# Norm roots and scalings of three mixers, placed between the difference heads of a two-layer attention stage

## The chip, the cores and the metric

The kernel runs on one core of a Trainium2 chip. The metric is the device time of one execution in microseconds (us); several runs are taken and their median counts. The engines are called as the profile calls them: PE is TensorE (PEld its weight loads), DVE is VectorE, ACT is ScalarE, POOL is GpSimd, SP is SyncE.

## The reference

Two transformer blocks run one after the other on 512 tokens of width 1024. The first (sparse attention, a recurrent branch, a gated feed-forward) is not touched by the change. The second is run twice (two layers); each layer has a half-weight gated feed-forward, a mixer stage, another feed-forward and a norm. In the mixer stage four kinds of attention work side by side on 256 columns each, and each result is normalised before one common projection:

```python
pa, pb, pc, pd = jnp.split(h @ w_in[l], IN_SPLITS, axis=-1)
ya = neighbourhood_mixer(pa, ...)   # rms_norm over its 256 columns
yb = mla_mixer(pb, ...)             # rms_norm over its 256 columns
yc = diff_mixer(pc, ...)            # rms_norm over the 64 columns of each head
yd = gqa_mixer(pd, ...)             # rms_norm over its 256 columns
x = x + jnp.concatenate([ya, yb, yc, yd], axis=-1) @ w_out[l]
```

`rms_norm` divides by `sqrt(mean(x*x) + eps)`. The difference mixer (`yc`) runs two softmaxes for each of its four heads and subtracts the second, weighted, from the first.

## The kernel before, in words

Tokens are in four blocks of 128 (`TB` = 4). The function `mixers` lays all attention of one layer out as 20 groups of 4 steps, 80 steps t = 0 to 79: four latent heads (groups 0 to 3), four neighbourhood heads (4 to 7), four shared-key heads (8 to 11), and eight groups for the difference heads (12 to 19, steps 48 to 79: two per head). A step is 128 queries against up to 512 keys. `attention` (from line 938 on) turns the list into one instruction stream per engine, by hand, with semaphores between them:

- PE, in its loop at t: the scores of step t + 4 (L967), the turning of step t's probabilities (L975, transposes), and the weighing of the values for step t - 2 (L986). Turning step t waits for its exponentials and for the copy of step t - 2.
- DVE: the scores' bias and row minimum (L1065) of step t, which waits for the exponentials of step t - 3; then what `splits(dve, t)` asks for; and at every fourth t, from t = 10 on, `finish` of a group: the reciprocal of the row sums (L1033), for a second softmax its weight (L1036), and the scaled output (L1047) into `ytok` (or into `sq` for a second softmax).
- ACT: the exponentials of step t (L1016), the copy of the turned probabilities of step t - 1 out of PSUM (L1023), and then what `on_act`, here the function `squares`, asks for at t.
- POOL adds the second softmax's part to the first in `ytok` (L1080).

`ytok` holds the 1024 output columns of the 512 tokens. The norms need three steps. ACT squares a mixer's output into the tile `nabias` (L2315, at t = 44, 46 and 60; L2320 for the difference heads 0 to 2, at t = 66, 74 and 80). DVE sums the squares into columns of the small tile `ms` (L2232, at the t of the table `sums`). Then the root (ACT), the reciprocal (DVE) and the scaling of `ytok` (DVE). Before the change the roots of the three 256-column mixers (L2324) stand at ACT's t = 80, behind the last square, and their reciprocals (L2236) and the three scalings (L2241, each over 4 x 256 columns) at DVE's t = 83, behind group 18's finish and ahead of group 19's, at t = 86. Behind them comes the last difference head: its square on DVE (L2333), its sum (L2335), the roots of all four heads on ACT (L2347), reciprocal, factor and the scaling of the difference mixer's 256 columns (L2337 to L2342).

`turn_outputs` then transposes `ytok` chunk by chunk on PE (L2771, 8 chunks of 4 blocks; the six chunks of the three mixers first, the two of the difference mixer last, by `Y_ORDER`), ACT writes the high part `yhi` (L2779, 8 instructions) and DVE the low part `ylo` (L2788, 14 instructions). The projection (`products`, L388 to L390: three matmuls per chunk) starts with the first chunk whose low part is there. PE's wait for a pair of chunks is `y_normed`, raised by each scaling:

```python
for i, c in enumerate(Y_ORDER):
    pe.wait_ge(*k.y_normed.at(i // 2 + 1))
```

ACT needs a table of functions for exponentials and another for roots; the compiler puts a load (ACT_TABLE_LOAD) ahead of an activation whose function is not in the table that is loaded. Squares and copies need no change of table here.

Of the kernel before, what the change touches and what calls it, by code (L numbers as in the profile page):

```python
# [21 lines left out]
ALU = mybir.AluOpType  # L22
# [39 lines left out]
GW = 256  # L62
# [1501 lines left out]
def spread(ap, n, at=None):  # L1564

    dims = [list(d) for d in ap.ap]
    dims.insert(len(dims) if at is None else at, [0, n])
    return bass.AP(ap.tensor, ap.offset, dims)
# [561 lines left out]
def mixers(k, mem, l, near, latent, diff, shared, parted, lam, ytok):  # L2130
# [4 lines left out]
    nc = k.nc  # L2135
# [78 lines left out]
    def splits(dve, t):  # L2214
        def parts(trios, done):
            for src, hi, lo in trios:
                last = nc.vector.tensor_copy(hi, src)
            last.then_inc(*k.part_hi.up())
            dve.wait_ge(*k.part_hi.all())
            for src, hi, lo in trios:  # L2220
                last = nc.vector.tensor_tensor(lo, src, hi.bitcast(F32), ALU.subtract)
            last.then_inc(*done.up())

        def latent_head(h):
            hi, lo, khi, klo = (x[0:MD] for x in slot[h % 2])
            parts([(qB[0:MD, h, :], hi, lo), (kB[0:MD, h, :], khi, klo)], k.latent_split)

        if t in sums:
            at, squares = sums[t]
            i = list(sums).index(t)  # L2230
            dve.wait_ge(*k.y_sq.at(i + 1))
            nc.vector.tensor_reduce(k.ms[:, :, at:at + 1], squares, AX.X, ALU.add).then_inc(*k.y_sums.up())  # L2232
        if t == 83:
            dve.wait_ge(*k.y_root.at(2))
            for at, size in ((0, 2), (6, 1)):
                last = nc.vector.reciprocal(k.ms[:, :, at:at + size], k.ms[:, :, at:at + size])  # L2236
            last.then_inc(*k.y_link.up())
            dve.wait_ge(*k.y_link.at(1))
            for at, col in ((0, 0), (1, GW), (6, 3 * GW)):
                y = ytok[:, :, col:col + GW]  # L2240
                nc.vector.tensor_tensor(y, y, spread(k.ms[:, :, at], GW), ALU.mult).then_inc(*k.y_normed.up())  # L2241
        if t == -1:
            latent_head(1)
        if t in (1, 4):
            dve.wait_ge(*k.qk_done.at(ends[0 if t == 1 else 1]))
            latent_head(2 if t == 1 else 3)
        if t in (5, 9):
            c = (t - 5) // 4
            parts([(kA[:, c, :], *near_keys[c])], k.keys_split)
        if t in (8, 12, 16, 20):  # L2250
            h = (t - 8) // 4
            dve.wait_ge(*k.qk_done.at(ends[2 + h]))
            r = 64 * (h % 2)
            parts([(qA[r:r + 64, h // 2, :], slot[h % 2][0][r:r + 64], slot[h % 2][1][r:r + 64])], k.padded)
        if t == 13:
            parts([(kD[:, :], *shared_keys)], k.keys_split)
        if t in (24, 28):
            v = (t - 24) // 4
            dve.wait_ge(*k.qk_done.at(ends[6 + v]))
            r = 64 * v  # L2260
            parts([(qD[r:r + 64, j, :], slot[v][2 * j][r:r + 64], slot[v][2 * j + 1][r:r + 64]) for j in range(2)],
                  k.padded)
        if t in (30, 48):
            c = 0 if t == 30 else 1
            hi, lo, khi, klo = diff_parts[c]
            parts([(qC[:, c, :], hi, lo), (kC[:, c, :], khi, klo)], k.parted)
# [41 lines left out]
    def squares(act, t):  # L2308
        if t in (44, 46, 60):
            i = (44, 46, 60).index(t)  # L2310
            at, done = ((GW, 4), (0, 8), (3 * GW, 12))[i]
            act.wait_ge(*k.o_read.at(done))
            if i == 0:
                act.wait_ge(*k.low_done.at(32))
            nc.scalar.activation(bias[:, :, i, :], ytok[:, :, at:at + GW], ACT.Square).then_inc(*k.y_sq.up())  # L2315
        if t in (66, 74, 80):
            h = (66, 74, 80).index(t)
            act.wait_ge(*k.o_added.at(h + 1))
            act.wait_ge(*k.y_sums.at(1))
            nc.scalar.activation(head(h), maps(h), ACT.Square).then_inc(*k.y_sq.up())  # L2320
        if t == 80:
            act.wait_ge(*k.y_sums.at(3))
            for at, size in ((0, 2), (6, 1)):
                nc.scalar.activation(k.ms[:, :, at:at + size], k.ms[:, :, at:at + size], ACT.Sqrt, scale=1.0 / GW,  # L2324
                                     bias=k.eps[:, 0:1]).then_inc(*k.y_root.up())

    attention(k, groups, mem, bias_ready=(4 * TB, na_ready), ready=ready, splits=splits, on_act=squares)

    @k.block.vector
# [729 lines left out]
```

## Time and profile before

| | |
|---|---|
| median of 3 runs | 3228.33 us (3226.97 to 3229.15) |
| profiled execution | 3228.01 us |
| its span in the trace | 3226.0 us |
| PE busy | 3149.0 us, 98% of the span |
| DVE busy | 1790.4 us, 55% |
| ACT busy | 1300.7 us, 40% |
| POOL busy | 215.1 us, 7% |

The span is the time between the first and the last instruction in the trace; the profiled execution's own time has 2.0 us more around it. An engine's busy share is an average over stages; PE's high share includes the time in which it runs at the lower of its two clock levels. Times in the trace are counted from the start of the span. The mixer stage of the first layer lies at about 1572 to 1728 us, that of the second at about 2653 to 2804 us.

### The profile page before, as it was taken

Reading aid. Unit: us, or ns where it says so; the run is one execution under the profiler, and the core shown is the slowest. Engines: PE = TensorE matmul, PEld = TensorE weight load, DVE = VectorE, ACT = ScalarE, POOL = GpSimd, SP = SyncE. Lnnn points to the kernel's source line nnn. Section 1 sums busy time; section 2 is a strip of 40 time slices with the busy share of each in tenths; the row PEclk is TensorE's granted clock in tenths of the full one; section 3 lists DMA queues with packets and bytes.
Section 4 is the critical chain, followed back from the end, with each engine's and each line's share of the span. In section 5 each row is a group of like instructions: output and inputs, shape, how many; then the busy total and the mean of one; then the engine's idle time right before and its main releaser. Section 6 shows DMA issues by size and latency. Waiting matters only on the chain.

```text
span 3226.0 us, 41165 instructions
## 1 busy us (share of the span) xinstructions
PE 3149.0 (98%) x15247; PEld 2603.0 (81%) x15247; DVE 1790.4 (55%) x2676; ACT 1300.7 (40%) x1857; POOL 215.1 (7%) x238
## 2 busy tenths in 40 slices
PE   8999998999999999999999999999999999999998
PEld 6779976888888888877788888888888768888887
DVE  8367696455543555347765555345553686555532
ACT  4337765233332333233365333333322426643322
POOL 1001100010000000011201000100000021000001
PEclk9999999999999999999999999999999999999999
DMA  5340033333333333343322333333333332233332
GB/s 148 87 129 5 2 92 105 94 93 100 94 94 100 92 102 91 100 115 78 68 51 73 94 96 96 97 97 97 91 97 99 104 83 40 64 94 102 92 96 67
DMA packets 520761, 283.71 MB, mean 88 GB/s; under 512 B 40139, under 2 KB 511024, under 8 KB 520371
## 3 DMA queue, kind: packets, MB, share of 16 engines
q1 hardware_dynamic: 513154, 262.77, 29.2%
q0 software_dynamic: 5088, 17.40, 1.8%
q10 hardware_dynamic: 2384, 1.71, 0.2%
q8 instruction: 88, 1.44, 0.2%
q14 instruction: 47, 0.38, 0.0%
HBM read 268.16 MB, written 4.24 MB: 84 GB/s over the span
## 4 chain that ended last, share of the span: by engine, by line
PE 88%; DVE 7%; issue 2%; ACT 2%; DMA 1%; ACTq 0%; DVEq 0%; POOLq 0%; POOL 0%
PE bank L388 24%; PE bank L389 24%; PE bank L390 24%; PE bank L986 5%; PE bank L967 4%; PE bank L975 3%; PE bank L2491 1%; DVE wlo L364 1%; PE bank L412 0%; DVE xc L1980 0%; DVE std L2690 0%; PE bank L413 0%; PE bank L414 0%; DVE ntmp L2680 0%; PE bank L743 0%
## 5 line engine op out<-in xcount | busy, mean ns | idle before, releaser
L388 PE MATMUL bank<-hhi,whi 128*128 128x512 f32 (+1 forms) x2440 | 973.7, 399 | 5.5 <-issue 2.5
L390 PE MATMUL bank<-hlo,whi 128*128 128x512 f32 (+1 forms) x2440 | 950.5, 390 | 0.0
L389 PE MATMUL bank<-hhi,wlo 128*128 128x512 f32 (+1 forms) x2440 | 949.9, 389 | 0.0
L364 DVE TENSOR_TENSOR wlo<-raw,whi 128x1024 fp32r<-128x1024 f32 x485 | 607.5, 1255 | 551.7 <-ACT whi L357 542.7
L357 ACT CAST whi<-raw 128x1024 fp32r<-128x1024 f32 x485 | 505.0, 1047 | 399.8 <-PE bank L390 379.8
L388 PEld LDWEIGHTS bank<-hhi,whi 128*128 128x128 f32 (+1 forms) x2440 | 457.1, 187 | 117.0 <-issue 18.6
L389 PEld LDWEIGHTS bank<-hhi,wlo 128*128 128x128 f32 (+1 forms) x2440 | 457.2, 187 | 106.0 <-issue 12.0
L390 PEld LDWEIGHTS bank<-hlo,whi 128*128 128x128 f32 (+1 forms) x2440 | 457.0, 187 | 97.2
L388 PE MATMUL bank<-uhi,whi 128*128 128x512 f32 x880 | 343.0, 390 | 0.0
L390 PE MATMUL bank<-ulo,whi 128*128 128x512 f32 x880 | 342.4, 389 | 0.0
L389 PE MATMUL bank<-uhi,wlo 128*128 128x512 f32 x880 | 342.4, 389 | 0.0
L650 ACT CAST uhi<-gate 128x512 f32 x110 | 68.3, 620 | 597.2 <-DVE gate L674 597.2
L667 DVE TENSOR_TENSOR up<-bank,rinv 128x512 f32<-128x512 f32 x110 | 76.0, 691 | 288.2 <-PE bank L390 288.2
L390 PEld LDWEIGHTS bank<-ulo,whi 128*128 128x128 f32 x880 | 165.2, 188 | 34.5
L388 PEld LDWEIGHTS bank<-uhi,whi 128*128 128x128 f32 x880 | 165.2, 188 | 34.4
L389 PEld LDWEIGHTS bank<-uhi,wlo 128*128 128x128 f32 x880 | 165.2, 188 | 33.9
L1023 ACT COPY probT<-bank 128x512 f32<-128x512 f32 (+3 forms) x288 | 140.4, 487 | 85.2 <-PE bank L975 83.6
L519 POOL TENSOR_TENSOR sq<-sq 128x512 f32<-128x512 f32 x49 | 63.4, 1293 | 1644.5 <-ACT sq L537 1644.5
L975 PE MATMUL bank<-ident,prob 128*128 128x128 f32 x896 | 147.1, 275 | 1.0 <-ACT prob L1016 0.6
L677 DVE TENSOR_TENSOR ulo<-gate,uhi 128x512 f32 x110 | 76.2, 693 | 99.5 <-ACT uhi L650 99.5
L975 PEld LDWEIGHTS bank<-ident,prob 128*128 128x128 f32 x896 | 112.2, 142 | 20.7 <-ACT prob L1016 3.7
L533 ACT ACTIVATE hhi<-xT,vec 128x512 fp32r<-128x512 f32 x48 | 34.7, 724 | 172.7 <-DVE xT L602 172.7
(457 smaller groups left out, 3689.0 us busy)
## 6 DMA issues: line engine op xcount, KB each, us to landing
raw<-in_ffn_w_gate SPq DMA_DIRECT2D x88, 512.0 KB, 3.8
raw<-in_ffn_w_up SPq DMA_DIRECT2D x88, 512.0 KB, 3.7
raw<-in_w_in SPq DMA_DIRECT2D x78, 512.0 KB, 3.7
raw<-in_ffn_w_down SPq DMA_DIRECT2D x64, 512.0 KB, 3.8
raw<-in_w_out SPq DMA_DIRECT2D x24, 512.0 KB, 4.0
raw<-in_ffn_w_down SPq DMA_DIRECT2D x32, 384.0 KB, 3.3
raw<-in_w_gate SPq DMA_DIRECT2D x22, 512.0 KB, 3.8
raw<-in_w_up SPq DMA_DIRECT2D x22, 512.0 KB, 3.6
```

What stands on the lines that cost most here:

```text
L357: k.nc.scalar.copy(k.whi[:, slot, :], k.raw[:, slot, :]).then_inc(k.hi_split.sem, 1)
L364: k.nc.vector.tensor_tensor(k.wlo[:, slot, :], k.raw[:, slot, :], k.whi[:, slot, :].bitcast(F32), ALU.subtract)\
L388: mm(out, whi, hi(kc), start=start and i == 0, stop=False)
L389: mm(out, wlo, hi(kc), start=False, stop=False)
L390: last = mm(out, whi, lo(kc), start=False, stop=stop and i == kcs - 1)
L650: nc.scalar.copy(uhi[:, bass.ds(i * 2 + e, 1), :], gate[:, e:e + 1, :])\
L667: nc.vector.tensor_tensor(up[:, e, :], bank[u + 1][:, :], k.rinv[:, :], ALU.mult)\
L677: nc.vector.tensor_tensor(ulo[:, bass.ds(i * 2 + e, 1), :], gate[:, e:e + 1, :], uhi[:, bass.ds(i * 2 + e, 1), :].bitcast(F32), ALU.subtract)\
L967: last = nc.tensor.matmul(score(t), q, key, start=i == 0, stop=i == len(pairs) - 1)
L975: last = nc.tensor.transpose(k.bank[4 + t % 2][:, b * P:b * P + P], prob[:, t % 2, b * P:b * P + P], k.ident[:, :])
L986: last = nc.tensor.matmul(mixed(g)[:, e, :], probT[:, t % 3, b * P:b * P + P], v, start=b == 0, stop=b == len(values) - 1)
L1023: nc.scalar.copy(probT[:, v % 3, 0:width[v]], k.bank[4 + v % 2][:, 0:width[v]])\
```

## The change

The roots of the three 256-column mixers go from ACT's t = 80 to t = 63 (the last of their sums is made at DVE's t = 61). The reciprocals go from DVE's t = 83 to t = 66, and the three scalings, which stood one behind the other, to t = 67, 71 and 75. No arithmetic is added or left out.

```diff
-        if t == 83:
+        if t == 66:
             dve.wait_ge(*k.y_root.at(2))
             for at, size in ((0, 2), (6, 1)):
                 last = nc.vector.reciprocal(k.ms[:, :, at:at + size], k.ms[:, :, at:at + size])
             last.then_inc(*k.y_link.up())
             dve.wait_ge(*k.y_link.at(1))
-            for at, col in ((0, 0), (1, GW), (6, 3 * GW)):
-                y = ytok[:, :, col:col + GW]
-                nc.vector.tensor_tensor(y, y, spread(k.ms[:, :, at], GW), ALU.mult).then_inc(*k.y_normed.up())
+        if t in (67, 71, 75):
+            at, col = ((0, 0), (1, GW), (6, 3 * GW))[(t - 67) // 4]
+            y = ytok[:, :, col:col + GW]
+            nc.vector.tensor_tensor(y, y, spread(k.ms[:, :, at], GW), ALU.mult).then_inc(*k.y_normed.up())
...
-        if t == 80:
+        if t == 63:
             act.wait_ge(*k.y_sums.at(3))
             for at, size in ((0, 2), (6, 1)):
                 nc.scalar.activation(k.ms[:, :, at:at + size], k.ms[:, :, at:at + size], ACT.Sqrt, scale=1.0 / GW,
```

Lines behind L2241 have a number higher by one in the changed kernel. The order of instructions is the same in both layers. ACT behind the square of the shared-key mixer (t = 60), first as it was, then as it is: L1016 are the exponentials of steps 61 to 64, L1023 the copies of steps 60 to 63.

```order
L2315 ACTIVATE nabias<-ytok 128x4x256 [waits o_read]
L1016 ACTIVATE prob<-biased,low 128x512 [waits low_done,p_turned]
L1023 COPY probT<-bank 128x512 [waits p_turned,pv_done]
L1016 ACTIVATE prob<-std,low 128x512 [waits low_done,p_turned]
L1023 COPY probT<-bank 128x512 [waits p_turned,pv_done]
L1016 ACTIVATE prob<-biased,low 128x512 [waits low_done,p_turned]
L1023 COPY probT<-bank 128x512 [waits p_turned,pv_done]
L1016 ACTIVATE prob<-biased,low 128x512 [waits low_done,p_turned]
L1023 COPY probT<-bank 128x512 [waits p_turned,pv_done]
```

In the changed kernel, from the copy of step 62 on:

```order
L1023 COPY probT<-bank 128x512 [waits p_turned,pv_done]
L2325 ACT_TABLE_LOAD
L2325 ACTIVATE ms<-ms,eps 128x4x2 [waits y_sums]
L2325 ACTIVATE ms<-ms,eps 128x4
L1016 ACT_TABLE_LOAD [waits low_done]
L1016 ACTIVATE prob<-biased,low 128x512 [waits p_turned]
L1023 COPY probT<-bank 128x512 [waits p_turned,pv_done]
```

Two roots and two table loads, one to the roots' table and one back, now stand between the copy of step 62 and the exponentials of step 64. ACT at the end of the attention, changed kernel:

```order
L2321 ACTIVATE nabias<-ytok 128x4x64 [waits y_sums,o_added]
L2345 UNCONDITIONAL_BRANCH
L2348 ACT_TABLE_LOAD
L2348 ACTIVATE ms<-ms,eps 128x4x4 [waits y_sums]
L2775 UNCONDITIONAL_BRANCH
L2780 ACTIVATE yhi<-bank,vec 128x4x8x16 [waits side_turned] x2
```

The load for the last roots stands ahead of the instruction that waits for the sums, and waits for nothing itself. Per layer ACT has two table loads more than before. DVE at the end of the attention, first as it was:

```order
L2232 TENSOR_REDUCE ms<-nabias 128x4 [waits y_sq]
L1033 RECIPROCAL scale<-bank 128x4 [waits pv_done]
L1047 TENSOR_TENSOR ytok<-bank,scale 128x4x64 [waits scale_ready]
L2236 RECIPROCAL ms<-ms 128x4x2 [waits y_root]
L2236 RECIPROCAL ms<-ms 128x4
L2241 TENSOR_TENSOR ytok<-ytok,ms 128x4x256 [waits y_link]
L2241 TENSOR_TENSOR ytok<-ytok,ms 128x4x256 x2
L1033 RECIPROCAL scale<-bank 128x4 [waits pv_done]
L1036 TENSOR_TENSOR scale<-scale,lam 128x4 [waits scale_ready]
L1047 TENSOR_TENSOR sq<-bank,scale 128x256 [waits o_added,factor_used]
```

And as it is:

```order
L2232 TENSOR_REDUCE ms<-nabias 128x4 [waits y_sq]
L1033 RECIPROCAL scale<-bank 128x4 [waits pv_done]
L1047 TENSOR_TENSOR ytok<-bank,scale 128x4x64 [waits scale_ready]
L1033 RECIPROCAL scale<-bank 128x4 [waits pv_done]
L1036 TENSOR_TENSOR scale<-scale,lam 128x4 [waits scale_ready]
L1047 TENSOR_TENSOR sq<-bank,scale 128x256 [waits o_added,factor_used]
L2330 UNCONDITIONAL_BRANCH
L2334 TENSOR_TENSOR nabias<-ytok 128x4x64 [waits o_added]
```

The finish of group 19 (L1033, L1036, L1047) now follows that of group 18 directly; the only thing between is its own wait for the weighed values.

## Rows read from the trace of the kernel before

**Rows 1.** The page: busy time of each engine.

```profile
PE 3149.0 (98%) x15247; PEld 2603.0 (81%) x15247; DVE 1790.4 (55%) x2676; ACT 1300.7 (40%) x1857; POOL 215.1 (7%) x238
```

**Rows 2.** The chain that ended last, end of layer 1's attention and projection: start, us, what.

```profile
1716.19 1.28 ACT L2324
1717.48 0.50 ACT ms L2324 x2
...
1718.29 3.50 DVE ytok L2241 x3
...
1725.13 1.24 DVE ytok L2342
...
1731.06 0.23 PE bank L388
```

**Rows 3.** Timeline of DVE, same place: start, us, engine, line, operation, out<-in.

```profile
1716.75 0.42 DVE L1047 TENSOR_TENSOR ytok<-bank,scale 128x256 f32<-128x256 f32 x1
...
1721.71 0.17 DVE L1033 RECIPROCAL scale<-bank 128x4 f32<-128x4 f32 x1
...
1726.27 6.10 DVE L2788 SCALAR_TENSOR_TENSOR ylo<-bank,vec,yhi 128x128 fp32r<-128x128 f32 x14
```

**Rows 4.** Timeline of PE, layer 1's end, then layer 2's; [idle before <- releaser].

```profile
1715.02 2.79 PE L986 MATMUL bank<-vC,probT 128*128 128x65 f32 x24
1719.57 4.37 PE L2771 MATMUL bank<-ident,ytok 128*128 128x128 f32 x24 [1.77 <-DVE ytok L2241]
1726.41 1.97 PE L2771 MATMUL bank<-ident,ytok 128*128 128x128 f32 x8 [2.47 <-DVE ytok L2342]
...
1734.30 0.39 PE L388 MATMUL bank<-yhi,whi 128*128 128x512 f32 x1
...
2795.91 3.36 PE L2771 MATMUL bank<-ident,ytok 128*128 128x128 f32 x24 [1.77 <-DVE ytok L2241]
...
2811.68 0.39 PE L388 MATMUL bank<-yhi,whi 128*128 128x512 f32 x1
```

**Rows 5.** Timeline of ACT, layer 1: copy of step 62, exponentials of step 64.

```profile
1690.28 0.56 ACT L1023 COPY probT<-bank 128x512 f32<-128x512 f32 x1
1690.74 0.72 ACT L1016 ACTIVATE prob<-biased,low 128x512 f32<-128x512 f32 x1
```

**Rows 6.** Timeline of PE, layer 1: scores of step 68, turning of step 64.

```profile
1691.93 0.48 PE L967 MATMUL bank<-hhi 128*128 128x512 f32 x1
1692.25 0.60 PE L975 MATMUL bank<-ident,prob 128*128 128x128 f32 x4
```

**Rows 7.** Timeline of ACT in the first block: a table load between other work.

```profile
445.57 1.28 ACT L1920 ACT_TABLE_LOAD   x1
446.87 0.69 ACT L1920 ACTIVATE tr<-bank,half 128x512 f32<-128x512 f32 x1
```

**Rows 8.** Timeline of PE: two gaps inside layer 1's attention.

```profile
1572.56 6.77 PE L967 MATMUL bank<-hhi 96*128 96x512 f32 x15 [2.38 <-DVEq L471]
...
1605.95 0.63 PE L967 MATMUL bank<-parted,hhi 128*128 128x256 f32 x3 [1.45 <-ACT prob L1016]
```

**Rows 9.** Windows: stretch, length, busy PE, PEld, DVE, ACT, POOL, PEclk, DMA share, GB/s.

```profile
219.00:220.40 1.40, 0.01 (x1) 0.00 (x0) 1.25 (x4) 0.71 (x2) 0.08 (x1) 1.00 0.46 187
220.40:226.00 5.60, 5.59 (x34) 4.67 (x34) 4.58 (x10) 2.19 (x4) 0.00 (x0) 1.00 0.01 3
1572.60:1580.00 7.40, 7.40 (x21) 5.79 (x22) 5.37 (x10) 1.39 (x3) 0.80 (x1) 0.54 1.00 223
1606.00:1611.00 5.00, 5.00 (x31) 5.00 (x31) 2.35 (x7) 2.79 (x6) 0.00 (x0) 0.66 0.01 3
1719.57:1723.90 4.33, 4.33 (x24) 4.13 (x24) 3.39 (x7) 0.00 (x0) 0.73 (x1) 0.63 0.00 0
1726.40:1730.00 3.60, 3.59 (x14) 3.21 (x15) 3.60 (x11) 3.60 (x6) 0.00 (x0) 0.56 0.02 5
2795.91:2799.30 3.39, 3.27 (x24) 2.57 (x24) 2.89 (x5) 0.00 (x0) 0.35 (x1) 1.00 0.00 0
```

## The prediction

> **What bounds the kernel.** I read the page first: PE is busy for 98% of the span and DVE for 55% [rows 1], so that a DVE or ACT instruction costs time only where PE waits for it. The change touches two such places in each of two layers. The chain of waits at the end of layer 1's attention shows the first [rows 2]: ACT's table load (1.28 us) and three-mixer roots (0.50), the three scalings on DVE (3.50), then group 19's finish, the last head's norm, and the last scaling (1.24), on which the last transposes wait. The timelines of DVE and PE [rows 3, 4] say what the other engines could do meanwhile. The second place is the middle of the difference heads, where the roots go; there the timelines of ACT and PE say how far ahead of PE the exponentials are [rows 5, 6]. Last I read windows for the granted clock behind PE's gaps [rows 8, 9], since both edits change a gap. Layer 2 repeats layer 1's instructions 1076.3 us later with the same durations; only the clock differs (its 24 transposes take 3.36 us against 4.37 [rows 4]).
>
> **The end of the attention: a gain.** Group 19's finish starts at 1721.71 behind the scalings [rows 3]. It needs the weighed values, whose matmuls end at 1715.02 + 2.79 = 1717.81 [rows 4], and DVE behind group 18's finish, free at 1716.75 + 0.42 = 1717.17 [rows 3]. With the scalings gone it starts at about 1717.87, **3.84 us earlier**, and everything behind it hangs on it: POOL's addition, the square, the sum, the root on ACT, the last scaling, the last eight transposes, and the low parts on DVE. Two things could be late instead. ACT must load the roots' table again, 1.28 us; the order shows that load without a wait ahead of the root that waits, so it runs from 1716.19 to 1717.47 in idle time, as the load does now [rows 2], while the last scaling starts at 1725.13 - 3.84 = 1721.29 [rows 2]. Without this cover it would cost 1.28. And PE must turn the first six chunks: they start at 1717.85, behind the weighing, and take 3.36 us (4.37 at the lower clock) [rows 4], so they end at 1721.2 (1722.2), before the last scaling's end at 1726.37 - 3.84 = 1722.53 [rows 2]. Both hide.
>
> **The middle: a cost.** After the copy of step 62, which ends at 1690.84 [rows 5], ACT loads a table (1.28), takes two roots (0.50) and loads the other table back [rows 2]. A load takes 1.30 from its start to the next start [rows 7], so the exponentials of step 64 start at about 1690.84 + 0.02 + 1.29 + 0.50 + 1.30 = 1693.95 instead of 1690.74 [rows 5] and end at 1694.67. PE turned step 64 at 1692.25, directly behind the scores of step 68 [rows 6]; it will now do so at about 1694.70. Of ACT's 3.2 us delay, 0.8 are its lead and **2.45 us** reach PE as a gap. PE works without gaps from there to the end of the weighing, so the shift stays. The reciprocals on DVE wait for the roots while DVE would wait for step 64's exponentials anyway; queued behind them are group 14's finish and the minimum of step 67, neither needed for several us. The three scalings (3.50 / 3 = 1.17 each) go one by one where DVE is ahead of ACT (its minimum of step t waits only for the exponentials of step t - 3); I cost them at nothing. That cover, the minima made ahead, would have to be gone for 1.17 each. Nothing moves on the DMA queues: SP's and POOL's streams are unchanged.
>
> **The clock.** In front of the middle the granted clock is at its upper level (2.4 GHz). What a gap does to it varies. Behind gaps of 2.38 and 2.47 us PE got 0.54 of full speed for 7.4 us and 0.56 for 3.6 us; behind one of 1.45, 0.66 for 5.0; behind 1.77, once 0.63 for 4.3 and once 1.00; behind 1.40, 1.00 [rows 4, 8, 9]. Lost work, (1 - clock) x length: 3.4, 1.6, 1.7, 1.6, 0, 0 us. My new gap of 2.45 is nearest to the first two; I take **1.7**, the value of three of those six (1.6 to 1.7), and keep 0 and 3.4 as the bounds. PE is the bound there, so it is paid in full.
>
> At the end the change removes the first gap (1.77) and shortens the second: from 1721.2 to 1722.55, 1.35 us. The nearest row, 1.40, left the clock up, so I take the upper level. What that gives back is capped by DVE: the low parts end 1726.27 + 6.10 = 1732.37 [rows 3], and the last chunk's three matmuls (0.23 each [rows 2]) would let the next unit start at 1733.1; it starts at 1734.30 [rows 4]. So 1.2 in layer 1. In layer 2, 1076.3 us later, the same point is 2809.4 against 2811.68 [rows 4]: 2.2. Bounds: 0 if the clock falls as before, and these values.
>
> **The sum.** Per layer -3.84 + 2.45 + 1.7 = +0.3 us; two layers +0.6; clock at the ends -1.2 - 2.2 = -3.4; in all -2.8 us. The profiled execution took 3228.01, so I expect **3225.2 us**. It stands 0.3 below the median of the runs shown, 3228.33, within their scatter. A measurement of this kernel tells about 0.2% (6.5 us) from no change; this is less.
>
> **A rule against the change.** The row of a load shows 1.28 us, and the activation behind it starts 1.30 after the load's start, in the middle of other ACT work [rows 7]. The Trainium skill, page "ScalarE: Activation LUTs", section "Table sets: the hidden batching unit", says to batch activations by table set and not by function, and the change breaks this: exponentials, roots, exponentials, roots. By the same page ("What ACT_TABLE_LOAD costs") a switch costs about 2.66 us with a drain; by that figure an estimate for the middle gap would be 5.2 us instead of 2.45, and two layers would come to +2.7. The trace's 1.30 decides; no row here shows the drain.
>
> **The rivals.**
>
> 1. *The clock stays up in the middle.* As behind 1.77 in layer 2. Then 2 x 1.7 less: -6.2, 3221.8; in one layer only, 3223.5. For it: the gap is short and the engine is dense around it. Against: both gaps of over 2.3 us had a fall behind them. 0.15 for both cases.
> 2. *The clock falls at the end too.* The weighing, the transposes and a 1.35 us gap lie close to the 1.45 that had a fall. The give-back shrinks from 3.4 to about 1.0 (the shorter gap still saves in layer 2): -0.4, 3227.6. 0.27.
> 3. *Slower: the middle costs more than the end gives.* Mechanism: the gap at step 64 puts PE at 1.2 GHz for as long as behind the 2.38 gap, 3.4 us of lost work, with the end's give-back at 1.0 as in rival 2. Per layer -3.84 + 2.45 + 3.4 = +2.0; in all +4.0 - 1.0 = +3.0, 3231.0. It turns from gain to loss once the lost work exceeds 3.84 - 2.45 = 1.39 us a layer plus what the end gives back. 0.12.
> 4. *A switch holds ACT longer than its load's row.* With a hold of twice the load's row (2 x 1.28 per switch, two switches), the gap is 2.45 + 2.57 = 5.0, and in all -2.8 + 5.1 = +2.3, 3230.3; with 3.4 of lost clock it would be 3233.7. Against it stand the 1.30 in the first block and the roots at 1717.48, directly behind the load [rows 2, 7]. This is what the skill's drain would do; 0.04.
> 5. *The end gives nothing.* If group 19's finish were held by something as late as the scalings (the chain names only them), the middle's cost would stand alone: 2 x 4.15 = +8.3, 3236.3. Nothing in the rows supports it: 0.02.
>
> **How the numbers follow.** The forecast as it stands has 0.40, the rivals 0.15, 0.27, 0.12, 0.04 and 0.02. The range goes from rival 1 (3221.8, rounded to 3222.0, since the half case is at 3223.5) to 3229.6: it takes in rival 2 and the forecast with the 1 us by which the runs scatter, and half of rival 3, and leaves out some 0.15. Faster by over 0.2%, below 3221.9, is rival 1's outer half: 0.06. Slower by over 0.2%, above 3234.8, is rival 5 and the worst of 3 and 4: 0.03. Within: 0.91.
>
> **What would show it.** In the changed profile: two table loads and two roots on ACT between a copy and an exponential in the middle; a PE gap of 2.4 to 2.5 us ahead of the turning of step 64, and a granted clock near 0.6 for some us behind it; group 19's L1033 starting about 1.1 us behind group 18's L1047 in place of 5.0; the gap of 1.77 ahead of the 24 transposes gone; the table load at ACT's end inside idle time. Wrong would be: a middle gap over 3 us (rival 4), the last root starting directly behind its table load (the cover is gone), or a stretch from the start of step 64's turning to the start of the projection that is not some 3.8 us shorter at equal clock.

## The result, and the profile after

The changed kernel takes **3232.46 us** in the median of 22 runs (3223.98 to 3251.21), against 3226.28 (3223.36 to 3232.93) of the kernel before in as many runs beside it: 1.0028 times as long, 95% interval 1.0015 to 1.0041. (The ratio with its interval is estimated from all the runs; that of the two medians is 1.0019. So it is with the ratios below.) That is slower by a small amount that the interval keeps clear of no change, where no measurable change was forecast, and the median lies outside the range given (3222.0 to 3229.6). The profiled execution of the changed kernel took 3239.04 us.

The page of the changed kernel, its span and the busy time of each engine, against [rows 1]:

```profile
span 3237.1 us, 41171 instructions
PE 3159.9 (98%) x15247; PEld 2612.9 (81%) x15247; DVE 1793.9 (55%) x2676; ACT 1306.3 (40%) x1861; POOL 215.9 (7%) x238
```

PE has the same 15247 matmuls and is busy for 10.9 us more. ACT has four instructions more (its four table loads, two a layer) and 5.6 us more. So the extra time is mostly in matmuls that run longer, not in waits.

First the place that the edit fills, the middle of layer 1's difference heads. ACT's timeline of the changed kernel (start, us, engine, line, operation, out<-in, count), against [rows 5]:

```profile
1688.00 0.57 ACT L1023 COPY probT<-bank 128x512 f32<-128x512 f32 x1
1688.59 1.28 ACT L2325 ACT_TABLE_LOAD   x1
1689.88 0.49 ACT L2325 ACTIVATE ms<-ms,eps 128x8 f32<-128x8 f32 x2
1690.39 1.28 ACT L1016 ACT_TABLE_LOAD   x1
1691.69 0.72 ACT L1016 ACTIVATE prob<-biased,low 128x512 f32<-128x512 f32 x1
```

And PE's timeline of it, against [rows 6] (the bracket is PE's idle time before the row, and what ended it):

```profile
1692.46 0.66 PE L975 MATMUL bank<-ident,prob 128*128 128x128 f32 x4 [2.32 <-ACT prob L1016]
...
1694.37 0.77 PE L967 MATMUL bank<-hhi 128*128 128x512 f32 x1
1694.94 1.05 PE L975 MATMUL bank<-ident,prob 128*128 128x128 f32 x4
...
1697.36 0.77 PE L967 MATMUL bank<-hhi 128*128 128x512 f32 x1
...
1700.34 0.77 PE L967 MATMUL bank<-hhi 128*128 128x512 f32 x1
```

The gap is 2.32 us. Behind it the scores take 0.77 in place of 0.48, four turnings 1.05 in place of 0.60, and from one step's scores to the next's it is 2.98 to 2.99 us (1694.37, 1697.36, 1700.34). Windows of the changed kernel say for how long: the two stretches behind the gaps (layer 1, layer 2), then the two stretches from the copy of step 62 to the copy of step 79.

```profile
1693.00:1710.10 17.10, 17.10 (x78) 16.01 (x77) 7.62 (x20) 7.93 (x14) 0.73 (x1) 0.50 0.33 94
2779.00:2792.70 13.70, 13.70 (x63) 12.79 (x63) 6.54 (x17) 5.89 (x12) 0.73 (x1) 0.52 0.38 113
1688.00:1723.68 35.68, 33.36 (x215) 31.52 (x215) 16.73 (x47) 23.44 (x41) 1.46 (x2) 0.76 0.22 60
2773.17:2807.22 34.05, 31.73 (x215) 30.01 (x215) 16.63 (x47) 23.43 (x41) 1.46 (x2) 0.80 0.23 63
```

The same two stretches in the kernel before, copy to copy:

```profile
1690.28:1715.27 24.99, 24.99 (x215) 24.07 (x215) 12.79 (x42) 20.40 (x36) 1.48 (x2) 1.00 0.32 86
2766.60:2791.60 25.00, 25.00 (x215) 24.08 (x215) 12.79 (x42) 20.42 (x36) 1.47 (x2) 1.00 0.31 85
```

The last three numbers of a row are the granted clock, the DMA share and the GB/s. The same 215 matmuls take 24.99 us at a clock of 1.00 before; afterwards PE is idle for 2.32 of 35.68 us and busy for 33.36, at 0.76 on average. During 17.1 us PE was busy without a pause and was granted 0.50 of full speed, the lower level (1.2 GHz). The middle cost 10.69 us in layer 1 and 9.05 in layer 2; the forecast was 4.15 in each.

Then the end of the attention. DVE's timeline of the changed kernel, the finishes of groups 18 and 19, against [rows 3]:

```profile
1725.15 0.42 DVE L1047 TENSOR_TENSOR ytok<-bank,scale 128x256 f32<-128x256 f32 x1
1726.25 0.18 DVE L1033 RECIPROCAL scale<-bank 128x4 f32<-128x4 f32 x1 [0.67 <-PE bank L986]
```

ACT's timeline there, the table load and the last roots, against [rows 2]:

```profile
1724.60 1.28 ACT L2348 ACT_TABLE_LOAD   x1
1728.84 0.31 ACT L2348 ACTIVATE ms<-ms,eps 128x16 f32<-128x16 f32 x1 [2.96 <-DVE ms L2336]
```

PE's timeline there and at the same place of layer 2, against [rows 4]:

```profile
1723.42 2.79 PE L986 MATMUL bank<-vC,probT 128*128 128x65 f32 x24
1726.05 2.79 PE L2772 MATMUL bank<-ident,ytok 128*128 128x128 f32 x24
1730.96 1.09 PE L2772 MATMUL bank<-ident,ytok 128*128 128x128 f32 x8 [2.12 <-DVE ytok L2343]
...
1737.95 0.39 PE L388 MATMUL bank<-yhi,whi 128*128 128x512 f32 x1
...
2814.51 1.09 PE L2772 MATMUL bank<-ident,ytok 128*128 128x128 f32 x8 [2.13 <-DVE ytok L2343]
...
2822.82 0.39 PE L388 MATMUL bank<-yhi,whi 128*128 128x512 f32 x1
```

Group 19's reciprocal starts 1.10 us behind group 18's L1047, where it was 4.96 [rows 3]; the load ends 2.96 us before the roots that need it; the 24 transposes follow the weighing with no gap and take 2.79 in place of 4.37 [rows 4]. From the copy of step 79 to the next unit of the projection it is 1737.95 - 1723.68 = 14.27 us, against 1734.30 - 1715.27 = 19.03: **-4.76**, with -5.04 forecast. In layer 2 it is 2822.82 - 2807.22 = 15.60 against 2811.68 - 2791.60 = 20.08: **-4.48**, with -6.04 forecast. In this pair of profiles the two middles cost 19.7 us where 8.3 were forecast, and the two ends gave 9.2 where 11.1 were. So most of what went wrong lies behind the middle gap, and a smaller part at the end, where the last gap is 2.12 and 2.13 us and not the 1.35 of the prediction.

### The profile page after: what moved, and what is told of

Same layout as the page of the kernel before. It is cut to its first block, busy times and chain, and to the rows that moved or that the text cites. A ratio compares the mean times of both kernels' runs of the same rounds, so it can differ in the third digit from the quotient of the medians.

```text
span 3237.1 us, 41171 instructions
## 1 busy us (share of the span) xinstructions
PE 3159.9 (98%) x15247; PEld 2612.9 (81%) x15247; DVE 1793.9 (55%) x2676; ACT 1306.3 (40%) x1861; POOL 215.9 (7%) x238
## 4 chain that ended last, share of the span: by engine, by line
PE 88%; DVE 7%; issue 2%; ACT 2%; DMA 1%; ACTq 0%; DVEq 0%; POOLq 0%; POOL 0%
PE bank L388 24%; PE bank L390 24%; PE bank L389 24%; PE bank L986 5%; PE bank L967 4%; PE bank L975 3%; PE bank L2492 1%; DVE wlo L364 1%; DVE xc L1980 0%; PE bank L412 0%; DVE std L2691 0%; PE bank L413 0%; PE bank L414 0%; ACT prob L1016 0%; PE bank L743 0%
## 5 line engine op out<-in xcount | busy, mean ns | idle before, releaser
L1023 ACT COPY probT<-bank 128x512 f32<-128x512 f32 (+3 forms) x288 | 140.5, 488 | 96.7 <-PE bank L975 94.6
```

The lines of the kernel that those rows point to most:

```text
L1023: nc.scalar.copy(probT[:, v % 3, 0:width[v]], k.bank[4 + v % 2][:, 0:width[v]])\
```

## The experiments

Two explanations were open. The theory: ACT's hold opens a gap on PE, and the clock behind it falls for longer than the prediction allowed; the gap decides, whatever opens it. The rival: the table switches, or the work moved to DVE, cost by themselves. Where a kernel does more than the kernel before, what it makes in addition is read by nothing.

**Other instructions in place of the change's.** The first four kernels: the roots on DVE, the roots moved alone, and ACT held by three squares or by one, with no change of table.

e1 starts from the kernel before and takes the three mixers' roots on DVE, by eight Heron steps on the 128 x 12 means at t = 65 to 72, and the scalings at t = 73, 76 and 79; ACT's roots at t = 80 are gone (the columns of `ms` are renumbered for it, which is left out here):

```diff
+        if 64 < t <= 64 + 8:
+            linked(nc.vector.reciprocal(step, guess))
+            linked(nc.vector.tensor_tensor(step, step, half, ALU.mult))
+            linked(nc.vector.scalar_tensor_tensor(out=guess, in0=guess, scalar=0.5, in1=step, op0=ALU.mult, op1=ALU.add))
...
+        if t in (73, 76, 79):
+            i = (73, 76, 79).index(t)
...
-        if t == 80:
...
-                nc.scalar.activation(k.ms[:, :, at:at + size], k.ms[:, :, at:at + size], ACT.Sqrt, scale=1.0 / GW,
```

> The changed kernel with the three mixers' roots taken on DVE (eight steps of Heron's iteration on 12 values a partition, one per step t = 65 to 72, scalings at t = 73, 76 and 79): the table switch in the middle is gone from ACT, the end of the attention is that of the change. Theory (the gap at step 64 brings PE's clock down, and it stays down for many steps): no gap, no low stretch in the middle, the whole gain at the end stays, 3.8 to 5 us in each layer: 7 to 11 us below before. Rival (scalings and small DVE work between the heads disturb the attention in themselves): within 3 us of the changed kernel, with the turning of the steps 65 to 80 late.

Measured: 3219.27 us (3216.48 to 3234.79, 6 runs) against 3227.65 (3221.05 to 3238.45, 18 runs): 0.9968 (0.9955 to 0.9981), faster. Without a hold of ACT in the middle a gain stays. It is 8.4 us in the medians; the prediction's two ends come to 11.1.

e2 is the kernel before with the roots alone moved; reciprocals and scalings stay at t = 83:

```diff
-        if t == 80:
+        if t == 63:
             act.wait_ge(*k.y_sums.at(3))
```

> The kernel before with only ACT's roots moved to t = 63; reciprocals and scalings stay at t = 83. So it has the middle's cost and almost nothing of the end's gain (the scalings no longer wait for the roots behind the last square: 1.1 us a layer). Theory: the whole loss is in the middle. From the medians, +6 for the change and about -9 for its two ends leave some +15 for two middles, so this kernel is 10 to 16 us slower than before. Rival (the gap alone, at 2.3 us a layer, with the low clock a matter of chance): +2 to +4.

Measured: 3240.26 (3236.35 to 3249.29, 6 runs), 1.0038 (1.0025 to 1.0051): the cost is that of the roots' place, without anything moved on DVE. e3 and e4 keep the roots where they were and hold ACT with squares whose result nobody reads, three of them (the cut shown) and one; e8, further down, has two:

```diff
+        if t == 63:
+            for tile in (qA, kA, qD, kC)[:3]:
+                nc.scalar.activation(tile[:, :, :], ytok[:, 0:2, 0:T], ACT.Square)
```

> The kernel before with three squares of 1024 elements a partition added on ACT at t = 63, written to tiles that nothing reads any more: ACT is held for about 3.0 us, as by the two roots and two table loads (3.1), with no table switched. Theory (it is PE's gap, whatever makes it): gap of about 2.2 us, low clock behind it, 10 to 16 us slower than before. Rival (the table switch does something beyond its time on ACT): +4 to +6 only, two gaps.

> The same with one square (1.06 us) in place of three: ACT's lead is 0.8 us, so a gap of about 0.2 us. Theory: the clock stays up, 0.4 to 1 us above before. Rival (any disturbance of ACT at t = 63 brings the low clock): above +5.

Measured: e3 3239.47 (3231.33 to 3246.85, 7 runs), 1.0035 (1.0021 to 1.0048); e4 3228.91 (3221.08 to 3246.37, 13 runs), 0.9996 (0.9985 to 1.0007). Timelines of PE in e2 and in e3, layer 1, where step 64 is turned:

```profile
1690.98 0.66 PE L975 MATMUL bank<-ident,prob 128*128 128x128 f32 x4 [2.32 <-ACT prob L1016]
```

```profile
1692.70 0.66 PE L975 MATMUL bank<-ident,prob 128*128 128x128 f32 x4 [1.94 <-ACT prob L1016]
```

Windows of e2 behind both gaps, then of e3:

```profile
1692.00:1698.80 6.80, 6.80 (x32) 6.27 (x32) 3.11 (x10) 3.84 (x8) 0.73 (x1) 0.52 0.79 233
2778.00:2798.50 20.50, 20.50 (x92) 19.22 (x92) 6.83 (x21) 8.92 (x16) 0.73 (x1) 0.51 0.27 78
```

```profile
1694.00:1704.20 10.20, 10.20 (x46) 9.47 (x46) 3.70 (x13) 4.75 (x9) 0.73 (x1) 0.51 0.53 157
2779.00:2792.70 13.70, 13.70 (x63) 12.79 (x62) 4.50 (x14) 6.55 (x12) 0.73 (x1) 0.51 0.41 120
```

e3 has no change of table in the middle and costs what e2 costs. The rival in which the switch itself costs, beyond the time for which it holds ACT, falls. The two rows of e2 show one more thing: the same gap in the same kernel and the same execution was followed by 6.8 us at half clock once and by 20.5 the other time.

**The gap filled, and gaps of other lengths and places.** e5 is the changed kernel with 20 transposes of the identity matrix on PE, ahead of the turning of step 64, where PE would wait:

```diff
         def turn(t):
+            if bias_ready and t == 64:
+                for _ in range(20):
+                    nc.tensor.transpose(k.bank[7][:, 3 * P:4 * P], k.ident[:, :], k.ident[:, :])
             pe.wait_ge(*k.exp_done.at(t + 1))
```

> The changed kernel with 20 transposes of the identity, 128 x 128, added on PE ahead of the turning of step 64, into PSUM columns that nothing reads: at 0.11 us each they fill 2.2 of the 2.3 us for which PE stands still there. ACT's hold and the 2.3 us of delay are as in the change. Theory (the stillness of PE brings the clock down): no low stretch in the middle; per layer -4.8 at the end and +2.3 in the middle: about 5 us below before, some 10 below the changed kernel's median. Rival (the low clock comes with the table switch or with the DVE scalings): as the changed kernel, 6 above before.

Measured: 3224.72 (3218.45 to 3236.22, 12 runs) against 3228.18 (3221.74 to 3243.92, 35 runs): 0.9997 (0.9984 to 1.001). PE's timeline of e5 in layer 1:

```profile
1688.59 2.35 PE L973 MATMUL bank<-ident 128*128 128x128 f32 x20
1691.08 0.66 PE L978 MATMUL bank<-ident,prob 128*128 128x128 f32 x4
```

Windows of e5 behind that place, layer 1 and layer 2:

```profile
1691.00:1708.00 17.00, 16.92 (x142) 16.21 (x143) 12.84 (x33) 14.24 (x27) 0.74 (x1) 1.00 0.35 103
2765.00:2782.00 17.00, 16.86 (x142) 15.91 (x140) 12.30 (x31) 14.24 (x26) 0.73 (x1) 1.00 0.38 109
```

ACT's hold and its two table loads are still there and step 64 is as late as in the changed kernel (its turning starts 4.46 us behind the copy of step 62 in both), but in 17 us PE now gets through 142 matmuls, where the changed kernel did 78 in 17.1. Only the idle time on PE is gone, and with it the fall of the clock and the slowdown.

The profile alone would be weak evidence: it is of the second fastest of twelve executions. But the granted clock is on record for every run (to 0.001, which is 3 us of one run's span, so only means over many runs tell something). Span times mean granted clock, averaged over the runs, is 3197.7 us for the change (22 runs), 3197.1 for the change again (e11, 12 runs) and 3197.8 for e5; the rest of the span, (1 - clock) x span, is 35.7, 33.1 and 25.8 us. So the three are equal but for the clock, and e5 loses 7.3 to 9.9 us less to the lower level. This is the experiment that shows the cause.

Two reservations: the gain against the kernel before was expected at 5 us and is 3.5 in the medians, with an interval that holds no change; and e5 was not measured beside the change, of which the second measurement (e11, 0.9992 to 1.0029) overlaps with e5's interval.

e6, e7 and e9 are the kernel before with one root of 128 numbers into a spare column of `ms`, which brings a load to the roots' table and one back: at t = 38 among the shared-key heads (e6), at t = 63 (e7), and at t = 38 with a square of 1024 elements behind it (e9). The cut shows e9's edit; e6 has its first two added lines alone, and e7 the same two at t = 63.

```diff
+        if t == 38:
+            nc.scalar.activation(k.ms[:, 0, 7:8], k.eps[:, 0:1], ACT.Sqrt)
+            nc.scalar.activation(qA[:, :, :], qC[:, :, :], ACT.Square)
```

> The kernel before with one root of a constant (one value a partition, to an unused column of ms) on ACT at t = 38, among the shared-key heads, which makes two table loads: ACT is held for about 2.9 us. A step there has three score matmuls in place of one. Theory with an addition (how long the clock stays low depends on how much PE computes per step): gap of about 2 us and a low stretch of the length seen behind the other gaps there, 3 to 7 us: 2 x (2 + 2.5) = +5 to +9. Rival (the low stretch is as long anywhere in the attention): as e7.

> The same root at t = 63, among the difference heads. Theory: as the three squares of e3, +10 to +14 us. If the two positions cost the same, the length of the low stretch does not hang on the heads.

> The kernel before with two squares of 1024 elements on ACT at t = 63: a hold of about 2.0 us, less a lead of 0.8: a gap of about 1.2 us, between e4's 0.2 and e3's 2.0. Theory: the low clock follows in some executions and not in others, so that the runs scatter; median +3 to +6. Rival (any gap counts alike): +10 or more in all runs.

Measured, against 3228.18: e6 3229.17 (3226.17 to 3243.62), 1.0011 (0.9998 to 1.0023); e7 3239.99 (3231.68 to 3258.14), 1.0033 (1.0014 to 1.0051); e8 3227.06 (3223.42 to 3238.09), 0.9998 (0.9984 to 1.0011), 12 runs each. PE's timelines at the place of the hold in layer 1, of e6, of e7 and of e8:

```profile
1649.85 0.97 PE L967 MATMUL bank<-parted,hhi 128*128 128x512 f32 x3 [1.37 <-ACT prob L1016]
```

```profile
1691.94 0.66 PE L975 MATMUL bank<-ident,prob 128*128 128x128 f32 x4 [2.01 <-ACT prob L1016]
```

```profile
1691.70 0.66 PE L975 MATMUL bank<-ident,prob 128*128 128x128 f32 x4 [0.99 <-ACT prob L1016]
```

Windows of e7 behind its two gaps, then of e8 behind its first:

```profile
1693.00:1703.20 10.20, 10.20 (x45) 9.47 (x45) 3.80 (x12) 5.00 (x9) 0.73 (x1) 0.50 0.53 157
2775.00:2778.40 3.40, 3.40 (x17) 3.22 (x16) 1.10 (x4) 1.92 (x4) 0.00 (x0) 0.50 0.76 211
```

```profile
1691.70:1702.00 10.30, 10.29 (x87) 9.87 (x87) 6.20 (x19) 8.66 (x16) 0.73 (x1) 1.00 0.64 175
```

Two switches cost nothing that can be measured where the gap is 1.37 us (e6) and 11.8 us in the median where it is 2.01 (e7), of which the gaps themselves are 4.0. In e6 and e8 both layers keep the clock up behind the gap (1.37 and 1.36, 0.99 and 0.99 us), so two expectations missed: e6 was to cost 5 to 9 us, e8 3 to 6. Between 1.37 and 1.94 us no gap was made.

e6 and e7 differ in the place and in the gap, so it could still be that the fall is long only among the difference heads. e9 makes the longer gap among the shared-key heads; e11 and e12 are the changed kernel and e1 again, measured side by side; e10 is e1 with 16 more transposes of the identity on PE in the gap before the last two chunks:

```diff
         for i, c in enumerate(Y_ORDER):
+            if i == 6:
+                pe.wait_ge(*k.o_read.at(19))
+                for _ in range(16):
+                    nc.tensor.transpose(banks[6][:, 3 * P:4 * P], k.ident[:, :], k.ident[:, :])
             pe.wait_ge(*k.y_normed.at(i // 2 + 1))
```

> e6 again (a root and two table loads on ACT at t = 38, among the shared-key heads), with one more square of 1024 elements there, to a tile that nothing reads any more. e6 left a gap of only 1.4 us there, since ACT's lead is larger, against 2.0 in e7, so the two could not be compared. ACT is now held for some 3.9 us, which should leave a gap of 2.3 us, as in the change. Theory (a low stretch among the difference heads lasts 3 to 20 us because their steps, with one score matmul, give PE little to compute; among the shared-key heads, with three, it ends sooner): gap 2.3 us and a low stretch of 3 to 7 us in each layer, +8 to +11 against before. Rival (the stretch is as long in any part of the attention): +12 or more, and stretches over 10 us in its profile.

> e1 (roots on DVE) with 16 transposes of the identity on PE ahead of the last two chunks, into a bank that they overwrite, so that PE is not still for the 2.1 us before the last scaling is done. If the clock falls there in some executions, this gives 1 to 2 us a layer in those: 0 to 3 us below e12. If the transposes run past the last scaling they cost up to 0.3 a layer.

> The changed kernel again, on the same chip as e9, e10 and e12: 4 to 8 us above before, with runs that scatter over 20 us.

> e1 again, on the same chip as the change: 7 to 11 us below before, 13 to 17 below the change.

Measured, 12 runs each against 3226.22 (3220.66 to 3253.47, 35 runs):

| kernel | median (lowest to highest), us | ratio (95% interval) |
|---|---|---|
| e9, gap of 2.3 at t = 38 | 3240.58 (3227.97 to 3252.21) | 1.004 (1.0025 to 1.0056) |
| e10, e1 with the end's gap filled | 3214.75 (3212.39 to 3229.72) | 0.9962 (0.9942 to 0.9982) |
| e11, the change again | 3233.37 (3221.27 to 3243.4) | 1.0011 (0.9992 to 1.0029) |
| e12, e1 again | 3220.87 (3216.49 to 3233.16) | 0.9982 (0.9965 to 0.9998) |

PE's timeline of e9 at the two holds:

```profile
1644.73 0.96 PE L967 MATMUL bank<-parted,hhi 128*128 128x512 f32 x3 [2.30 <-ACT prob L1016]
...
2722.41 1.62 PE L967 MATMUL bank<-parted,hhi 128*128 128x512 f32 x3 [2.32 <-ACT prob L1016]
```

Windows of e9 behind them:

```profile
1644.73:1655.00 10.27, 10.27 (x76) 9.36 (x76) 3.17 (x6) 6.36 (x12) 0.00 (x0) 1.00 0.09 21
...
2722.50:2726.00 3.50, 3.50 (x15) 3.12 (x15) 1.79 (x4) 1.95 (x4) 0.00 (x0) 0.51 0.32 75
```

In this profile one gap had no fall behind it and the other a short one. But the profiled execution was the fastest of the twelve (3227.97; the next is 3232.05), and the median is 14.4 us above the kernel before, of which the two gaps are 4.6. The clocks of the twelve runs give (1 - clock) x span = 35.9 us, 5.1 more than the kernel before beside them; reckoned in the same way e2, e3 and e7, with their gaps among the difference heads, lose 6.8, 6.5 and 7.3 more. So falls came here too, in other runs than the profiled one, and the idea that they come only among the difference heads is not supported; whether they are somewhat shorter here stays open. The median is where the rival was expected (12 or more above), the loss of clock nearer to the theory.

e11 has the median 7.2 us above the kernel before, as the first measurement had (6.2), though its interval by itself reaches 0.9992: its runs scatter over 22 us. e12 is 5.4 us below the kernel before, where 7 to 11 were expected, and 12.5 below e11, where 13 to 17 were. e10 is the fastest kernel made, 11.5 us below the kernel before and 6.1 below e12. PE's timeline of e10 at the end of layer 1's attention:

```profile
1716.16 2.79 PE L2782 MATMUL bank<-ident,ytok 128*128 128x128 f32 x24
1718.79 1.91 PE L2777 MATMUL bank<-ident 128*128 128x128 f32 x16
1721.07 1.09 PE L2782 MATMUL bank<-ident,ytok 128*128 128x128 f32 x8 [0.38 <-DVE ytok L2349]
1722.20 0.47 PE L388 MATMUL bank<-yhi,whi 128*128 128x512 f32 x1
```

PE's timeline of e12 at the same place:

```profile
1720.02 1.09 PE L2778 MATMUL bank<-ident,ytok 128*128 128x128 f32 x8 [2.13 <-DVE ytok L2349]
1721.14 0.47 PE L388 MATMUL bank<-yhi,whi 128*128 128x512 f32 x1
```

The projection starts equally far behind the start of the last transposes in both (1.13 and 1.12 us): the added transposes shorten no wait of the program. PE's idle time goes from 2.13 to 0.38 us. The clocks of the runs agree that what they give is clock: span times clock is 3194.0 us for e10 and 3192.5 for e12, and the rest of the span 21.7 and 28.2. Where all of it is saved is not shown. 0 to 3 us were expected, the two intervals overlap, and in e12's profile layer 2 has 3.4 us at half clock behind that gap and layer 1 none; in e10's neither has any.

## Why the prediction was wrong

**What bounds the kernel** held: PE, with DVE and ACT counting where PE waits.

**The end, -3.84 per layer, right as to the waits.** Group 19's finish followed group 18's by 1.10 us in place of 4.96, the table load fell into idle time, and the 24 transposes were done before the last scaling. The low parts on DVE end 3.84 us sooner behind the copy of step 79 (1736.94 - 1723.68 against 1732.37 - 1715.27).

**The middle gap, 2.45, right.** It was 2.32 in both layers. Load to root was 1.29 us (1688.59 to 1689.88) and load to exponentials 1.30 (1690.39 to 1691.69), the number read from [rows 7]; rival 4's longer hold did not show. The Trainium skill, page "ScalarE: Activation LUTs", section "What ACT_TABLE_LOAD costs", has about 2.66 us for a switch with its drain; these rows differ from it, and no drain is in them. Its advice to batch by table set (section "Table sets: the hidden batching unit") was right at t = 63, where the hold reached PE (e7), and worth nothing that can be measured at t = 38 (e6); what costs is the hold, since e3 costs as much with no load at all. The scalings on DVE cost nothing: no wait of PE is put down to them. e2, which leaves them at t = 83, stands 12.6 us above the kernel before, the changed kernel 6.2 and 7.2; in e2 group 19's reciprocal starts 4.02 us behind group 18's L1047 (1718.79 to 1722.81), so 0.94 of the 3.84 is there already, and the difference of 5.4 to 6.4 fits the 2 x (3.84 - 0.94) = 5.8 that moving the scalings is worth beyond it.

**The clock, 1.7 us of lost work a layer with bounds 0 and 3.4, is the step that failed.** Layer 1's stretch was 17.1 us at 0.50, layer 2's 13.7 at 0.52: 8.6 and 6.6 us of lost work. Over the ten gaps of 1.94 to 2.33 us in the middle, in five profiles, the stretches behind them at half clock lasted:

| kernel | gap, us | layer 1, us | layer 2, us |
|---|---|---|---|
| the change | 2.32 | 17.1 | 13.7 |
| e11, the change again | 2.32 | 3.4 | 17.1 |
| e2, roots alone | 2.32, 2.33 | 6.8 | 20.5 |
| e3, three squares | 1.94 | 10.2 | 13.7 |
| e7, one root | 2.01, 2.02 | 10.2 | 3.4 |

Their mean is 11.6 us, and at about 0.51 this is 5.7 us lost a layer. That is too high for a typical run, since four of the five profiled executions lie above their kernel's median, three of them by 4.2 to 6.6 us. From the clocks of all runs it is less: the change and e11 lose 9.9 and 7.3 us more than e5, and e2, e3 and e7 lose 6.8, 6.5 and 7.3 more than the kernel before, which is 3.3 to 5.0 a layer. The two middles of the change then cost 2 x 2.32 + 7.3 to 9.9 = 11.9 to 14.5 us, and the two ends alone give 8.4 or 5.4 (the medians of e1 and e12): +3.5 to +9.1, where 6.2 and 7.2 were measured. This is rival 3's mechanism, and its turning point, 1.39 us of lost work a layer plus what the ends give, was passed; its price, 3.4, was near the mean over the runs and far below the two stretches of the profile.

The error was in how the price was read. The six rows behind it came from one execution and from other places (a phase of products, the start of a head), with clocks of 0.54 to 0.66 (means over windows that hold some time at full clock too), and I took their spread for the spread of the quantity. Three runs of the kernel before within 2.2 us seemed to say that the clock repeats. It doesn't: one kernel gave 6.8 and 20.5 us behind the same gap. The changed kernel's runs show it as well: 3223.98 us at a mean granted clock of 0.992 (below the median of the kernel before), 3239.04 at 0.988. So chances of 0.12 for rival 3 and 0.03 for slower were too small, since the upper bound of the worst term rested on one row.

**The give-back at the ends, 3.4 us for both layers, was sized wrong too.** The last gap was put at 1.35 us, next to a row of 1.40 with no fall; it is 2.12 and 2.13. The 3.36 us for the 24 transposes was read from a row in which they are paced by the three scalings: with these done they take 2.79, and PE waits the longer. In the profile of the change the clock stayed up behind this gap in layer 1 and not in layer 2, where 3.4 us at half clock start at 2816 (the kernel before has 6.8 from 2802 on). Over the five profiles with this end (the change, e11, e12, e1, e5) five of the ten gaps had a fall behind them, each of about 3.4 us. This is rival 2, which had 0.27. With the ends alone, e1 and e12 stand 8.4 and 5.4 us below the kernel before, short of the 11.1 forecast; with the last gap filled as well, e10 reaches 11.5.

## What to carry to other kernels

A wait of ACT or DVE that reaches PE costs the gap and what the clock does behind it, and the second part can be the larger: here 2.3 us of gap cost 2.3 and on average 3 to 5 more. So before work is moved from the end into a stream that feeds PE, see whether it opens a gap there that was not there before; if it must, fill the gap with matmuls whose result is not used (e5, e10), or take the work off the engine that PE waits for (three small roots on DVE by Heron's iteration, e1). And a term that differs from execution to execution needs several profiles and a dozen runs or more; three runs close together prove nothing.

## What the runs showed of the hardware that was not expected

- The clock stayed at its lower level while PE was busy without a pause: 17.10 of 17.10 us in the changed kernel, 20.50 of 20.50 in e2. What ends such a stretch, and why the same program has 3.4 us of it in one execution and 17.1 in the next, was not found.
- Gaps of 0.99 and 1.37 us (e8, e6) brought no fall at their place, ten of 1.94 to 2.33 in the middle all did, of two more of 2.30 and 2.32 at t = 38 one did, and of ten of 2.12 and 2.13 at the end of the attention five did. So the length of a gap alone does not decide; behind the end's gaps the stretches were short (3.4 us), in the middle up to 20.5. Why was not tried.
- A cast of 64x512 on DVE (L2217, in the latent heads, untouched by any edit) is of uneven length. In the kernel before its median over eight is 0.42 us and its longest 2.10; in e4 and in e1 one of them took 4.04 and 4.12. The rows of e4, DVE, POOL and PE, with PE's window behind the gap:

```profile
1591.40 4.04 DVE L2217 CAST hhi<-qA 64x512 fp32r<-64x512 f32 x1 [3.03 <-PE bank L967]
...
1587.56 7.60 POOL L2170 TENSOR_TENSOR nabias<-ytok 128x256 f32<-128x256 f32 x11
...
1597.59 1.65 PE L967 MATMUL bank<-hhi 96*128 96x512 f32 x3 [2.92 <-ACT prob L1016]
...
1597.00:1631.00 34.00, 33.41 (x148) 32.22 (x148) 13.74 (x32) 12.17 (x24) 1.98 (x2) 0.51 0.00 1
```

The eleven additions of POOL shown end at 1595.16 and the cast at 1595.44; in the kernel before the cast of 2.10 lies beside a memset of POOL of 1.80. The exponentials wait for DVE, PE waits 2.92 us for them, and 34 us at half clock follow. At 0.51 these are 16.7 us of lost work, which is what lies between e4's profiled execution (3245.57) and its median (3228.91). In e1's profile 27.3 us at half clock follow the long cast. It is seen in two of the fourteen profiles, so it may be one source of the scatter. That the cast is long because POOL works beside it was not tried, and can't be all: the cast of the same place in the kernel before (1593.21) also lies beside POOL's additions and took 0.69.
